# An expert mixer whose tokens are fetched by an indirect DMA from a copy of h, and whose results are added to h pair by pair

## The reference

```python
def hierarchical_moe(h, w_group, b_group, w_expert, b_expert, w_gate_up, w_down):
    ...
    g_prob, g_idx = lax.top_k(group_probs, 1)
    ...
    e_prob, e_local = lax.top_k(jax.nn.softmax(in_group, axis=-1), TOP_K_IN_GROUP)
    ...
    gates = g_prob * e_prob
    expert_ids = g_idx * EXPERTS_PER_GROUP + e_local
    ...
    def expert_block(args):
        xb, e = args
        g, u = jnp.split(xb @ w_gate_up[e], 2, axis=-1)
        return (jax.nn.silu(g) * u) @ w_down[e]
...
    for i in range(DEPTH):
        ...
        h = h + mix
        h = h + hierarchical_moe(rms_norm(h, norm_ffn[i]), ...)
    return rms_norm(h, final_norm)
```

## Time and profile before

| | us |
|---|---|
| median of 3 runs (lowest, highest) | 1338.35 (1338.27, 1340.99) |
| span of the profiled execution | 1339.6 |
| PE busy, share of the span | 1281.9, 96% |
| DVE busy | 498.7, 37% |
| ACT busy | 311.7, 23% |
| POOL busy | 148.9, 11% |

### The profile page before, as it was taken

One profiled execution on the slowest core, in us unless ns is written; L12 is line 12 of the kernel. 1 busy time (PEld: TensorE's weight loads), 2 busy tenths in 40 slices (PEclk: granted clock), 3 DMA queues, 4 the chain that ended last, 5 costly groups with the idle time before them and its releaser, 6 DMA issues.

```text
span 1339.6 us, 15996 instructions
## 1 busy us (share of the span) xinstructions
PE 1281.9 (96%) x6188; PEld 687.6 (51%) x6188; DVE 498.7 (37%) x1178; ACT 311.7 (23%) x622; POOL 148.9 (11%) x122
## 2 busy tenths in 40 slices
PE   7999999999999998989999999999999999999896
PEld 5777664444444433334588888744444444433342
DVE  5586342223222322224656662432223222322235
ACT  3267611111111111111443321211111111111103
POOL 4950120000000000000000002200001000000000
PEclk9999989999999999999999999899999999999999
DMA  9901569999999999999823336689999999999997
GB/s 347 342 8 60 255 259 419 429 427 428 429 427 429 428 428 426 428 427 426 257 88 105 103 142 267 250 347 427 427 428 428 427 428 428 429 426 428 426 428 296
DMA packets 68579, 462.53 MB, mean 345 GB/s; under 512 B 18020, under 2 KB 33406, under 8 KB 43956
## 3 DMA queue, kind: packets, MB, share of 16 engines
q1 hardware_dynamic: 63232, 452.87, 81.6%
q0 software_dynamic: 4800, 7.96, 1.6%
q10 hardware_dynamic: 500, 1.06, 0.2%
HBM read 443.40 MB, written 26.24 MB: 351 GB/s over the span
## 4 chain that ended last, share of the span: by engine, by line
PE 75%; DMA 21%; DVE 2%; ACT 0%; issue 0%; SPq 0%; POOLq 0%; DVEq 0%
PE ps L1170 22%; PE ps L962 20%; PE ps L1188 13%; DMA big<-in_moe_w_gate_up_dram 12%; PE ps L1145 8%; DMA small<-in_moe_w_gate_up_dram 6%; DMA big<-rows 2%; PE ps L1160 2%; PE ps L1179 1%; PE ps L926 1%; PE ps L1105 1%; PE ps L1271 1%; PE ps L1154 1%; PE ps L1044 1%; PE ps L1011 1%; PE ps L945 1%
## 5 line engine op out<-in xcount | busy, mean ns | idle before, releaser
L1170 PE MATMUL ps<-big,arena 128*64 128x512 f32 x976 | 218.2, 594 | 17.1 <-DMA big<-in_moe_w_gate_up_dram 15.6
L1685 DVE SCALAR_TENSOR_TENSOR gain<-ps,slot_root,arena 64x512 f32<-64x512 f32 x64 | 72.8, 1137 | 403.1 <-ACT arena L810 402.1
L617 POOL DMA_INDIRECT rows<-arena x60 | 59.0, 983 | 827.7 <-DVE arena L1713 827.7
L1170 PEld LDWEIGHTS ps<-big,arena 128*64 128x64 f32 x976 | 68.9, 137 | 158.4 <-issue 131.1
L810 ACT ACTIVATE arena<-ps,slot_root 64x512 f32<-64x512 f32 x64 | 43.7, 682 | 452.6 <-PE ps L1170 452.6
L1170 PE MATMUL ps<-small,arena 128*64 128x512 f32 x496 | 111.9, 593 | 5.1 <-DMA small<-in_moe_w_gate_up_dram 5.1
L962 PE MATMUL ps<-xt_parts,small_parts 128*128 128x512 f32 x288 | 110.6, 393 | 0.0
L962 PE MATMUL ps<-xr_parts,small_parts 128*128 128x512 f32 x272 | 105.9, 389 | 0.0
L1188 PE MATMUL ps<-big,arena 128*64 128x512 f32 x432 | 98.7, 598 | 1.5 <-DMA big<-in_moe_w_down_dram 1.5
L962 PE MATMUL ps<-xt_parts,big_parts 128*128 128x512 f32 x256 | 99.7, 389 | 0.0
L1170 PEld LDWEIGHTS ps<-small,arena 128*64 128x64 f32 x496 | 35.4, 137 | 77.0 <-issue 68.3
(11 more groups left out here) (218 smaller groups left out, 1687.7 us busy)
## 6 DMA issues: line engine op xcount, KB each, us to landing
big<-in_moe_w_gate_up_dram SPq DMA_DIRECT2D x61, 2048.0 KB, 27.9
small<-in_moe_w_gate_up_dram SPq DMA_DIRECT2D x31, 2048.0 KB, 28.6
big<-in_moe_w_down_dram SPq DMA_DIRECT2D x27, 2048.0 KB, 30.1
arena<-in_moe_w_gate_up_dram SPq DMA_DIRECT2D x16, 2048.0 KB, 30.1
small<-in_moe_w_down_dram SPq DMA_DIRECT2D x11, 2048.0 KB, 28.7
xt<-in_moe_w_gate_up_dram SPq DMA_DIRECT2D x10, 2048.0 KB, 25.4
h<-in_moe_w_gate_up_dram SPq DMA_DIRECT2D x10, 2048.0 KB, 24.7
xt<-in_moe_w_down_dram SPq DMA_DIRECT2D x10, 2048.0 KB, 31.8
```

What stands on the lines that cost most here:

```text
L617: nc.gpsimd.indirect_dma_start(out=rows_dram[l], out_offset=bass.IndirectOffsetOnAxis(ap=where[:, j:j + 1], axis=0), in_=S.y_rows[:, j, :] ...
L1170: mm = nc.tensor.matmul(ps[2 + j][half * BLOCK:(half + 1) * BLOCK, :], S.xg[:, k, j * BLOCK:(j + 1) * BLOCK], w[:, a, half * FF:(half + 1) ...
L1685: V.scalar_tensor_tensor(out=hid[BLOCK:P, j, :].rearrange("q (k p) -> q p k", p=P), in0=ps[2 + j][BLOCK:P, :].rearrange("q (p k) -> q p k" ...
```

## The change

The scatter to DRAM, the zeroing of its target, the load of all rows and the split of h go. In their place:

- POOL stores h to DRAM (`h_dram`, 2 MB a layer) as its four token tiles are finished, and clears `picked` once a layer. h itself stays in SBUF through the stage, so the ring takes `xr` as a slot and not `h`; the order of its slots changes.
- Rows in: four narrow products (`index`, 68 columns and not 4) fetch for each slot the token number, 1/rms and the gates of all experts. DVE makes an index (`find_index`), slot_root and slot_gate. POOL issues an indirect DMA (`gather`) that brings the 4 KB rows of h into `picked`; slots without a token are out of bounds and skipped. `turn_picked` and `take` follow as before.
- Rows out: ACT and DVE scale an expert's rows by their gates into a high and a low part (`take_high`, `take_low`). PE spreads the ranks over the partitions (`spread`), DVE compares them with the slot numbers (`find_slots`), which is the selection transposed, and `combine` multiplies it with the rows: 32 products a pair, 64 partitions deep, with the two halves of the columns alternating. DVE adds them to h (`add`).
- The adding of a pair is spread over the next pair's order on PE in four parts, one token tile each. The last pair's 32 products follow its down.
- The loop over pairs is written out instead of run as a loop. The router builds a table (`tab`) and PE transposes the ranks once a layer (`turn_ranks`).

```diff
-        ring = [[halves[1][0], small[:, 0], halves[0][1], halves[0][0], late_slot, halves[1][1], small[:, 1], xt_slot, h[:]],
-                [*halves[1], halves[0][0], late_slot, small[:, 1], halves[0][1], small[:, 0], xt_slot, h[:]]]
+        ring = [[halves[1][0], small[:, 0], halves[0][1], halves[0][0], late_slot, halves[1][1], small[:, 1], xr[:], xt_slot],
+                [*halves[1], xr[:], halves[0][0], late_slot, small[:, 1], halves[0][1], small[:, 0], xt_slot]]
...
+            def gather(S, l, i, slot, taken):
+
+                pool.wait_ge(S.index_ready, i + 1)
+                if taken is not None:
+                    pool.wait_ge(S.picked_turned, taken)
+                pool.sem_inc(mark, 1)
                 nc.gpsimd.indirect_dma_start(
-                    out=rows_dram[l], out_offset=bass.IndirectOffsetOnAxis(ap=where[:, j:j + 1], axis=0),
-                    in_=S.y_rows[:, j, :], in_offset=None,
-                    bounds_check=2 * NONE - 1, oob_is_err=False).then_inc(S.scattered[j], 16)
+                    out=picked, out_offset=None, in_=h_dram[l],
+                    in_offset=bass.IndirectOffsetOnAxis(ap=where[:, slot:slot + 1], axis=0),
+                    bounds_check=T - 1, oob_is_err=False).then_inc(S.picked_in, 16)
...
+            def combine(t, js, bank, start, stop):
+
+                for j in js:
+                    for y in (y_high, y_low):
+                        for c in range(2):
+                            rows = slice(c * BLOCK, (c + 1) * BLOCK)
+                            mm = nc.tensor.matmul(ps[bank + c][:], parts(selT[rows, j, t * P:(t + 1) * P]),
+                                                  parts(y[rows, j, :]), start=start and j == js[0] and y is y_high,
+                                                  stop=stop and j == js[-1] and y is y_low)
+                return mm
...
+                for t in range(TT):
+                    add(S, o + LAST, t, 2 * t, h_ready)
+                dve.wait_ge(h_ready, 2 * TT * (l + 1))
                 dve.wait_ge(route_ready, l + 1)
-                most = dve.value_load(fullest[0:1, 0:1], min_val=0, max_val=T)
+                most = dve.value_load(fullest[0:1, l:l + 1], min_val=0, max_val=T)
```

More of the change, by code:

```diff
@@ L225, in build_trunk @@
         gain_in = sem("gain_in")
[L226 removed]
+        router_in = sem("router_in")
         wr_scaled = sem("wr_scaled")
@@ L634, in _ @@
-                pool.wait_ge(cleared, 16 * L)
-                with pool.Fori(0, LAST) as i:
-                    for j in range(2):
-                        scatter(S, l, j, i)
+                    nc.gpsimd.dma_start(h_dram[l][t * P:(t + 1) * P, :], h[:, t, :]).then_inc(h_stored, 16)
+                if l == 0:
+                    pool.wait_ge(o_ps, U)
+                    pool.wait_ge(pT_ready, 4 * U)
+                else:
+                    pool.wait_ge(conv_ready, DT)
+                nc.gpsimd.memset(picked, 0.0).then_inc(pool_step, 1)
@@ new lines, in experts @@
+                                    down(O, q * 2 + j, j, small[:, j])
+                                pe.wait_ge(over_masked[l], q + 1)
+                                for j in range(2):
+                                    mm = nc.tensor.matmul(ps[j][:], ones[0:E, :], over_ranks[0:E, j, :],
+                                                          start=True, stop=True)
+                                mm.then_inc(O.spread, 1)
+                                pe.wait_ge(O.selT_ready, q + 1)
@@ new lines, in find_index, with find_sums @@
+            def find_index(S, slot):
+                V.tensor_scalar(where[:, slot:slot + 1], ps[5][:, INDEX:INDEX + 1], -1.0, float(NONE),
+                                ALU.mult, ALU.add).then_inc(S.index_ready, 1)
+            def find_sums(out, slot, cols, done):
+                for j in range(2):
+                    for c in range(2):
+                        row = ps[5][j * BLOCK:(j + 1) * BLOCK, :]
+                        a, b = (INDEX + col for col in cols(j))
+                        ins = V.tensor_scalar(out[c * BLOCK:(c + 1) * BLOCK, slot, j:j + 1], row[:, a:a + 1],
+                                              row[:, b:b + 1], None, ALU.add)
+                ins.then_inc(done, 1)
@@ L1828, in experts @@
+                                find_slots(O, q)
+                                for t in range(TT):
+                                    add(O, q, t, 2 * t, O.added)
+                            dve.wait_ge(O.added, r * (PAIRS * TT))
+                            dve.sem_inc(mark, 1)
                         with dve.Else():
```

736 lines of the change are left out of this document (314 added, 422 removed).

## The result

| | before | after |
|---|---|---|
| time, median | 1338.31 us (1338.22 to 1340.99) | 1354.99 us (1353.07 to 1356.76) |
| ratio to before | | 1.012 (95% interval 1.0105 to 1.0135) |
| span of the profiled execution | 1339.6 | 1353.6 |
| first product on weights, layer 0 | 195.65 | 198.89 |
| layer 0, from there to the end of the last down | 448.6 | 459.4 |

The changed kernel is 1.2% slower, 17 us where no change was forecast, and 3 us beyond the range. The spans differ by 14.0 us, and the table says where they are: +20.0 in the two stages, +3.2 at the first start, -8.9 at the two ends, -0.3 between. (Wherever a run lists both, its time stands 1.5 to 1.9 us above its span. By that, the execution profiled before the change took about 1341.3, 3 us above its median, and these 3 us of the 17 are not in the comparison of the spans.)

What follows compares the result with a forecast made beforehand. Weight transfers were taken to bound both expert stages, with air on TensorE. Stages 0, starts +4.5, ends -4 and -1 sum to -0.5 us: span 1339.6 to 1339.1, median forecast 1338, range 1328 to 1352.

Steps and rivals of the forecast that it cites:

- TensorE inside the stage: Both expert stages: pair goes from 27.13 to 27.85 us, stage 440, below 448.6, so 0 us change.
- The sum: TensorE's work per pair: 27.13 less pick 3.87, plus spread 0.48 and combine 4.11, giving 27.85 us.
- Transfers bound the stage before, with air for TensorE: Expert stages of the kernel before: transfers set 448.6 us, PE needs 429, leaving 20 us of air, 1.2 a pair.
- the sum's threshold of 28.4: Pair time in an expert stage above which transfers no longer hide TensorE's work; 0.5 us of stalls a pair free.
- Bytes in the stage: DMA in the expert stages: scatters out, 10.7 us a layer, gathers in, 9.8; counted at 0 to -1 a layer.
- Stalls: Inside a pair: PE waits four times for DVE's adds, but DVE has only 15 us of work in 27.9.
- the tightest place: Under a pair's first weight piece of 3.43 us: DVE's find_slots, take_low and select take 2.8, 0.3 to 0.6 spare.
- Rival (B): Expert stages: PE becomes the bound through ordered hand-overs inside a pair; likeliest 1344 to 1356 us, chance 0.22.
- The Trainium skill's rule: Combine's alternating row halves: products in different row groups overlap, so each costs half a pick product, 0.12 us, pair 27.6.
- Gathers: Row gathers after a stage's first: land in 8 to 10 us, hidden with 8 us to spare before turn_picked.
- Starts: Start of each expert stage, waiting for the first gather: +3 us in layer 0, +1.5 in layer 1, together +4.5.
- Ends: After each stage's last down: layer 0 from 22.2 to about 18 us, -4; layer 1 from 16.3 to 15.2, -1.

Runs made afterwards that it cites:

- the last experiment: Changed kernel with each part of combine made of 4 products over all 128 rows instead of 8 over 64, four places kept: 1361.1 us, ratio 1.0174.

## Why the prediction was wrong

**TensorE inside the stage: the failing step.** The sum gave a pair of 27.85 us and 0.5 of air below 28.4. It measured 28.95. Term by term, from the chain:

| | forecast | measured |
|---|---|---|
| combine, 32 products | 32 x 0.1285 = 4.11 | 1.13 + 1.12 + 1.12 + 1.13 = 4.50, which is 32 x 0.115 + 4 x 0.20 |
| spread | 0.48 | 0.65 |
| the four pieces of gate and up | 13.73, unchanged | 4 x 3.58 = 14.32 |
| together | 18.32 | 19.47 |

That is 1.15 more, less some hundredths elsewhere. The product was even cheaper than its nearest row. What the sum had no term for is the change of kind (of the weight tile's size, as the last experiment tells): 0.20 us for a group of other products whatever its number, and 0.15 in the piece behind it. The change takes one group out (pick), puts five in (four of combine, one of spread), and adds four places a pair (two before, six now), one after each of the first three pieces and one at the pair's end. One of the two prices was in my own rows: in the earlier trace rows the pieces that come behind their like, or behind down, take 3.43 (13.73 / 4), and those behind other products 3.58. I read both numbers and kept 13.73.

**Transfers bound the stage before, with air for TensorE: right,** as the added products in the kernel before show, though the air was 1.0 to 1.1 us a pair and not 1.2. The measured pair lies 0.55 us above the sum's threshold of 28.4. The threshold held to 0.1: where TensorE had room the changed transfers took 450 us a stage, which gives (450 + 5.6) / 16 = 28.5. And the sum itself was sound but for its terms: with 28.95 in it, 16 x 28.95 - 5.6 = 457.6, against 457.3 measured in layer 1 and 459.4 - 2.2 = 457.2 in layer 0. **Bytes in the stage,** put at 0 to -1, cost some 1.3 to 1.6 us a layer where they could be seen.

**Stalls: right in kind.** Inside a pair TensorE waits for no add of VectorE's, also not at the tightest place. Rival (B) had the outcome and the size (28.95 lies between its 28.7 and 29.4, 1348 and 1370), but its mechanism, ordered hand-overs, was not it; "4 more changes between kinds of products", which stood under it as a remark, was. A chance of 0.22 was too low for a case whose price I had not looked for.

**The Trainium skill's rule** ("TensorE: Matmul & The Clock Gate", "Part 3: Packing small matmuls — row/col tiling"), that products in different row groups run at the same time: by it a product in the new order would have been 0.12, and the part measures 0.115 a product. But with the halves not in turn it is the same, so no run here shows that the turns bring it. The prediction counted the 4.1 us of L1247 for the rule; those products did not take turns either, so they spoke against the turns.

**Gathers: right.** Hidden after the first, though at 10.5 us and not 8 to 10. The Trainium skill's figure ("DMA: Bandwidth & Descriptors", "Anatomy of one DMA — SWDGE (gpsimd) path"), an estimate of 2.6 us, was met by none: the fastest of 32 took 4.2, with the others behind weights in the queues.

**Starts.** Layer 0 +3.2 as forecast (+3), and 2.2 besides for the first piece at half clock, which the sum lacked although it charged just that at the other end. Layer 1 -0.3 in this profile, not +1.5; but the same stretch was 0.3 to 2.8 us longer than before in the other runs on the changed kernel, so one profile doesn't decide it.

**Ends.** Layer 0 -6.7, not -4: at the end the granted clock was 1.00 from 654 to 674 us, so the 1.5 for the low clock fell away, and TensorE turned the first tiles while the last were still being added. Layer 1 -2.2 and not -1.

## What to carry to other kernels

Where a stage has little air, count the places at which the engine leaves its main stream of products, not only the products: here 0.35 us a place, as much as three of the products put there, and the same 32 products in half as many groups gave back four fifths of the loss. Part of the price is readable beforehand, by comparing a block that comes behind its like with one that doesn't. And before paying for a shorter end of a transfer-bound stage, ask what its start does to the transfers: here one undid the other.

## What the runs showed of the hardware

- Between products with a weight tile of `128*64` and products with another one, TensorE lost 0.20 us in the group of others and 0.15 in the block behind it, whether the others were 64 rows deep (0.20 + 0.115 a product) or 128 (0.20 + 0.23 a product). Where neighbours had the same size of tile, the loss was not there: four transposes of `64*128` took 0.24 us behind products of `64*128`, and 0.39 behind products of `128*64` or `128*128`.
- A product 64 rows deep with 512 columns took half the time of one 128 deep, in either order of the row halves (1.12 and 1.14 us for eight).
- An indirect gather of 256 KB on average, with full queues, landed in 10.5 us (median), the scatters in 8.0; with one 2 MB piece of weights fewer issued ahead of it the first one took 4.1 us instead of 7.3.
- The granted clock fell to 0.50 with TensorE busy (193 us in the changed kernel, some time behind an idle stretch of 1.64 us), and stayed at 1.00 through stretches of 1.8 and 1.7 us at the end of the same stage. Between the layers it cost 3.3 to 7.0 us from one execution to the next.
